# Norm sums collected while the residual is made, no meetings of the engines around norms, gate rows loaded aside, and one build of the rotation tables, in a three-block model kernel

## The chip, the cores and the metric

The kernel runs on one core of one Trainium2 chip. Five engines work side by side and meet only through semaphores: TensorE (PE, matrix products and transposes into PSUM), VectorE (DVE), ScalarE (ACT, which also starts the small loads), GpSimd (POOL, here mostly a queue of DMA starts) and SyncE (SP, here only the queue of weight loads). The metric is device microseconds for one execution. Less is better.

## The reference, cut to what matters

x is 1024 rows (time) by 1024 columns, float32. It passes three blocks. Between the large products stand norms over the 1024 columns of each row: five of the plain kind and three of the layer kind.

```python
def rmsnorm(x, g):                       # norm_g[0], norm_g[1], final_g, norm_w_3, final_norm_w_3
    return x * lax.rsqrt(jnp.mean(x * x, -1, keepdims=True) + 1e-6) * g

def _layer_norm(x, g, b):                # ln_in, ln1, ln2
    mu = jnp.mean(x, -1, keepdims=True)
    var = jnp.mean(jnp.square(x - mu), -1, keepdims=True)
    return (x - mu) * lax.rsqrt(var + 1e-5) * g + b

# block 1: an S5 mixer, then an SGU mixer
h = rmsnorm(x, norm_g[0]); branch, gate = split(h @ s5_w_in)
y = gelu(s5_mixer(branch, ...)); y = y * sigmoid(y @ s5_w_glu + b)
x = x + (y * silu(gate)) @ s5_w_out
h = rmsnorm(x, norm_g[1]); u, v, gate = split(h @ sgu_w_in)
x = x + (sgu_mixer(gelu(u), gelu(v), ...) * silu(gate)) @ sgu_w_out
x = rmsnorm(x, final_g)
# block 2
h = _layer_norm(x, ln_in_g, ln_in_b)
mix = concat([gated_delta(h @ w_in), forgetting_attention(h @ w_in)]) @ w_out
h = _layer_norm(ALPHA * h + mix, ln1_g, ln1_b)
ff = square(relu(h @ w_up)) @ w_down
ple = (p @ w_ple) * sigmoid(h @ w_ple_gate + b)
h = _layer_norm(ALPHA * h + ff + ple, ln2_g, ln2_b)
# block 3
h = _rmsnorm(h, norm_w_3); parts = h @ w_in_3 + b_in_3
x = h0 + concat([hgrn2(parts), gla(parts), mlstm(parts)]) @ w_out_3   # h0: what block 2 gave
out = _rmsnorm(x, final_norm_w_3)
```

In the S5 mixer a complex diagonal state of 64 groups is carried through time. The kernel does it with a real scan of blocks of 8 steps, for which the inputs are turned by powers of a unit complex number before the scan and turned back after it. These powers, 128 for each of 32 pairs of groups, are the rotation tables.

## The kernel before

All work is written out in order for each engine. The program is a list of 26 phases (from line 3167), and every engine runs its part of phase 1, then of phase 2, and so on. After every phase but the last stands `meet` (line 3190): each of the four computing engines drains, raises `phase_end`, and waits until all four have raised it. ACT starts the small loads of a phase first, then does its work in it (lines 3217 to 3220). SP alone runs ahead: it fills a ring of 8 weight blocks, waiting only for the product that frees a slot.

The residual stream lies in `c.X` as 8 tiles of 128 columns by 1024 rows, transposed (columns on partitions), so a mean over columns is a product with `mean_mat`, a 128x128 matrix of 1/1024. Products come as groups: `product_ct` (line 150) makes one tile of 128 columns by 1024 rows out of 8 tiles of input, 16 calls of 512 rows each. Each call shows as two matmul records in the trace, so a group is 32 records. There are two PSUM slots for groups. PE waits for a slot by `group_read`, the readers wait by `group_done`, and `taken` waits until a reader has read a group. The trace names `c.X` residual, `c.B` normed, `c.C` gate, `c.D` and the scratch areas work, `c.row` row.

`norm_phase` (line 196) is used for all eight norms. Plain kind: ACT squares tile k into one of two scratch tiles (line 230), PE multiplies it with `mean_mat`, summing over the 8 tiles in one PSUM group (line 220, 32 records), ACT makes the inverse root as exp(-0.5 ln) in `inverse_root` (lines 182 and 185, with a table load for each function), DVE scales all 8 tiles (line 248). Layer kind: PE first makes the mean the same way (line 213, 32 records), DVE copies it out of PSUM (line 240) and subtracts it tile by tile (line 243), then follow squares, sum, root and scaling as above, and DVE adds the bias in a second pass (line 253).

Ahead of a norm a phase makes the residual tile by tile: `load_phase` (transposes of x, copied out of PSUM by ACT and DVE in turn), `add_to_residual` (line 778, once per product group), `mix_phase` (line 1838) and `ff_phase` (lines 1932 to 1936). `rows3_phase` (line 1963), a phase of its own behind the last norm of block 2, loads 70 rows of gate parameters with 18 DMAs, turns them with one transpose and does six tiny steps.

The S5 mixer: `s5_input_phase` makes `branch` in 8 groups while DVE prepares parameters; `s5_scan_phase` (line 473) then makes 8 chunks of 8 groups of channels. In each chunk DVE builds two operand sets (lines 633 to 655, signal `s5_pq_done`), then the rotation table `E` of the chunk by doubling (lines 657 to 687), then, once PE has made `X` (line 574), turns, scans and turns back (lines 702 to 722, signal `s5_h_done`). PE in each chunk: transposes (line 554), kernel (line 566), `X` (line 574), one group of the gate product (line 158), then `y` (lines 584 and 586), which waits for `s5_h_done` and for a matrix that POOL sends through memory. ACT copies `y` out (line 606) before PE may begin the next chunk.

Of the kernel before, what the change touches and what calls it, by code (L numbers as in the profile page):

```python
# [16 lines left out]
P = 128  # L17
# [132 lines left out]
def product_ct(c, pe, g, blocks, acts):  # L150
# [12 lines left out]

def product_tc(c, pe, g, blocks, acts, tile):
# [3 lines left out]
    for q in range(0, len(blocks), 4):  # L168
# [4 lines left out]
        for k in range(KT):  # L173
            last = pe.matmul(out[:, q * P:q * P + BANK], acts[k][:, tile * P:(tile + 1) * P], wide[:, :, k, :],  # L174
# [12 lines left out]

def columns(c, w, first, count, k0=0, kt=KT):
# [7 lines left out]
def norm_phase(c, src, dst, gain, bias, eps):  # L196
# [3 lines left out]
    layer = bias is not None  # L200
    g_mean = c.plan.groups if layer else None
    c.plan.groups += 2 if layer else 1
    g_sq = c.plan.groups - 1
    scratch = c.tmp
    base = c.norms
    c.norms += 1

    def tensor(pe):
        if layer:
            out = start_group(c, pe, g_mean)  # L210
            for k in range(KT):
                for h in range(HALVES):
                    last = pe.matmul(out[:, h * BANK:(h + 1) * BANK], c.mean_mat[:, :],
                                     src[:, k, h * BANK:(h + 1) * BANK], start=(k == 0), stop=(k == KT - 1))
            last.then_inc(c.group_done, 1)
        out = start_group(c, pe, g_sq)
        for k in range(KT):
            pe.wait_ge(c.square_ready, KT * base + k + 1)
            for h in range(HALVES):
                last = pe.matmul(out[:, h * BANK:(h + 1) * BANK], c.mean_mat[:, :],  # L220
                                 scratch[:, k % 2, h * BANK:(h + 1) * BANK], start=(k == 0), stop=(k == KT - 1))
            last.then_inc(c.square_used if k < KT - 1 else c.group_done, 1)

    def scalar(act):
        for k in range(KT):
            if layer:
                act.wait_ge(c.centred, KT * c.layer_norms[g_sq] + k + 1)
            if k >= 2:
                act.wait_ge(c.square_used, (KT - 1) * base + k - 1)
            act.activation(scratch[:, k % 2, :], (dst if layer else src)[:, k, :], ACT.Square).then_inc(c.square_ready, 1)  # L230
        inverse_root(c, act, take_group(c, act, g_sq), bias=eps).then_inc(c.group_read[g_sq % 2], 1)

    if layer:
        c.layer_norms[g_sq] = len(c.layer_norms)

    def vector(dve):
        chain = c.dve_chain
        if layer:
            mean = take_group(c, dve, g_mean)
            chain.done(dve.tensor_copy(c.row[:, :], mean), c.group_read[(g_mean) % 2], (g_mean) // 2 + 1)  # L240
            chain.wait()
            for k in range(KT):
                dve.tensor_tensor(dst[:, k, :], src[:, k, :], c.row[:, :], ALU.subtract).then_inc(c.centred, 1)
            dve.wait_ge(c.centred, KT * (c.layer_norms[g_sq] + 1))
        taken(c, dve, g_sq)
        a = dst if layer else src
        for k in range(KT):
            chain.done(dve.scalar_tensor_tensor(dst[:, k, :], a[:, k, :], gain[:, k:k + 1], c.row[:, :],
                                                ALU.mult, ALU.mult))
        if layer:  # L250
            chain.wait()
            for k in range(KT):
                chain.done(dve.tensor_scalar(dst[:, k, :], dst[:, k, :], bias[:, k:k + 1], None, ALU.add))

    return Phase(tensor=tensor, scalar=scalar, vector=vector)


# [11 lines left out]
def load_phase(c, x):  # L269
# [20 lines left out]

    def scalar(act):
        for k in range(0, KT, 2):
            act.activation(c.X[:, k, :], take_group(c, act, g0 + k), ACT.Copy)\
               .then_inc(c.group_read[(g0 + k) % 2], 1)

    def vector(dve):
        dve.wait_ge(c.rows_turned, 1)
        dve.tensor_copy(c.vecs[:, 0:c.n_vector_rows], c.pb[:, 0, 0:c.n_vector_rows])
# [3 lines left out]
    return Phase(loads=loads, tensor=tensor, scalar=scalar, vector=vector)  # L302


def s5_input_phase(c, t):
# [38 lines left out]
    def tensor(pe):  # L344
# [4 lines left out]
        for m in range(KT):  # L349
            product_ct(c, pe, g0 + m, [(b0 + m, KT, P)], [c.B[:, k, :] for k in range(KT)])  # L350
# [118 lines left out]

    return Phase(loads=loads, tensor=tensor, scalar=scalar, vector=vector, gpsimd=gpsimd)  # L470


def s5_scan_phase(c, t):
# [30 lines left out]
    E = area(2, JC, S5_N)  # L504
# [84 lines left out]
    def scalar(act):  # L589
        for i in range(S5_C):  # L590
# [11 lines left out]
            act.activation(c.C[:, i, :], take_group(c, act, g0 + i), ACT.Silu).then_inc(c.group_read[(g0 + i) % 2], 1)  # L602
            act.wait_ge(c.s5_y_done, i + 1)
            if i >= 1:
                act.wait_ge(c.s5_y_stored, 16 * S5_T * i)
            act.activation(Y.rearrange("p (j e) n -> p e j n", e=2), c.pb[:, 2:4, :].rearrange("p e (j n) -> p e j n", j=JC), ACT.Copy)\
               .then_inc(c.s5_y_read, 1)

    def vector(dve):
# [7 lines left out]
        for i in range(S5_C):  # L617
# [4 lines left out]
            tmp = T.rearrange("p c j n -> p (c j n)")  # L622
            if i >= 1:
# [33 lines left out]
            ch.wait()  # L657
            ch.done(dve.memset(E[:, 0, :, 0:1], 1.0))
# [2628 lines left out]
```

## Time and profile before

| | us |
|---|---|
| median of 3 runs | 4812.77 |
| lowest, highest | 4812.63, 4816.57 |
| the profiled execution | 4816.69 |
| its span, first to last instruction | 4815.0 |
| PE busy in the span | 4298.4 (89%) |
| DVE, ACT, POOL busy | 1412.4, 850.3, 251.0 |
| mean granted TensorE clock | 0.93 of full |

In a row of the instructions in order of time stand: start and length in us, engine, line, operation, result<-operands, sizes, how many were merged. In brackets at the end is the idle time of that engine just before it and the engine and line that ended it. `DVEq L3193` or `ACTq L3193` is the `drain` of a `meet`. A granted clock of 1.00 is 2.4 GHz, 0.50 is 1.2 GHz.

### The profile page before, as it was taken

Reading aid. Unit: us, or ns where it says so; the run is one execution under the profiler, and the core shown is the slowest. Engines: PE = TensorE matmul, PEld = TensorE weight load, DVE = VectorE, ACT = ScalarE, POOL = GpSimd, SP = SyncE. Lnnn points to the kernel's source line nnn. Section 1 sums busy time; section 2 is a strip of 40 time slices with the busy share of each in tenths; the row PEclk is TensorE's granted clock in tenths of the full one; section 3 lists DMA queues with packets and bytes.
Section 4 is the critical chain, followed back from the end, with each engine's and each line's share of the span. In section 5 each row is a group of like instructions: output and inputs, shape, how many; then the busy total and the mean of one; then the engine's idle time right before and its main releaser. Section 6 shows DMA issues by size and latency. Waiting matters only on the chain. (4 is left out here: it accounts for less than half of the span.)

```text
span 4815.0 us, 32872 instructions
## 1 busy us (share of the span) xinstructions
PE 4298.4 (89%) x13735; PEld 2208.2 (46%) x13735; DVE 1412.4 (29%) x2443; ACT 850.3 (18%) x945; POOL 251.0 (5%) x368
## 2 busy tenths in 40 slices
PE   6888698999879899977989999999969999889787
PEld 3455343444344577444434444444425555444443
DVE  3388201210133454133110000000234553312432
ACT  2111101200125121243000000000032430210122
POOL 0133000000000122021000000000000000000000
PEclk9878799999979999988999999999989999979898
DMA  3122111111001111100111111111101001011000
GB/s 106 60 49 54 60 35 40 44 31 40 26 10 35 36 31 31 48 31 14 31 35 40 39 36 39 39 32 30 44 18 27 27 9 40 7 40 56 21 9 37
DMA packets 287985, 172.98 MB, mean 36 GB/s; under 512 B 24047, under 2 KB 278878, under 8 KB 287582
## 3 DMA queue, kind: packets, MB, share of 16 engines
q1 hardware_dynamic: 248848, 124.86, 9.3%
q0 software_dynamic: 9856, 23.87, 1.9%
q10 hardware_dynamic: 29134, 22.14, 1.5%
q8 instruction: 110, 1.80, 0.2%
q14 instruction: 37, 0.30, 0.0%
HBM read 157.63 MB, written 13.21 MB: 35 GB/s over the span
## 5 line engine op out<-in xcount | busy, mean ns | idle before, releaser
L158 PE MATMUL products<-normed,weights 128*128 128x512 f32 x2176 | 953.7, 599 | 46.5 <-ACT normed L748 36.5
L158 PE MATMUL products<-residual,weights 128*128 128x512 f32 x1696 | 736.3, 595 | 19.7 <-DVEq L3193 18.8
L158 PEld LDWEIGHTS products<-normed,weights 128*128 128x128 f32 x2176 | 416.3, 192 | 569.6 <-issue 561.0
L158 PE MATMUL products<-gate,weights 128*128 128x512 f32 x1408 | 613.9, 596 | 18.8 <-POOLq L3193 7.6
L158 PEld LDWEIGHTS products<-residual,weights 128*128 128x128 f32 x1696 | 323.3, 191 | 426.8 <-issue 403.3
L158 PEld LDWEIGHTS products<-gate,weights 128*128 128x128 f32 x1408 | 269.1, 191 | 360.9 <-issue 337.6
L2224 PE MATMUL products<-normed,weights 128*128 128x512 f32 (+1 forms) x672 | 306.4, 606 | 1.6 <-DVEq L3193 1.6
L2224 PEld LDWEIGHTS products<-normed,weights 128*128 128x128 f32 (+1 forms) x672 | 123.3, 190 | 148.3 <-issue 145.2
L174 PE MATMUL products<-weights,normed 128*128 128x512 f32 x384 | 167.6, 599 | 13.4 <-DVEq L3193 13.4
L614 DVE TENSOR_TENSOR work<-work 128x4 f32<-128x4 f32 (+9 forms) x592 | 171.4, 289 | 21.6 <-DVE work L661 0.5
L230 ACT ACTIVATE work<-residual 128x1024 f32<-128x1024 f32 x64 | 67.1, 1055 | 538.6 <-DVEq L3193 305.1
L220 PE MATMUL products<-work,mean_mat 128*128 128x512 f32 x256 | 123.9, 646 | 41.8 <-ACT work L230 41.8
L3003 POOL DMA_DIRECT2D out_dram<-work x8 | 4.3, 538 | 2564.0 <-ACT work L2992 2560.4
L781 DVE TENSOR_TENSOR residual<-products,residual 128x1024 f32<-128x1024 f32 x32 | 39.2, 1225 | 301.5 <-PE products L158 301.5
L174 PEld LDWEIGHTS products<-weights,normed 128*128 128x128 f32 x384 | 73.7, 193 | 106.9 <-issue 92.6
L2303 PEld LDWEIGHTS others<-work 128*128 128x128 f32 (+1 forms) x1024 | 94.4, 195 | 47.3 <-issue 37.9
L1497 PE MATMUL products<-residual,weights 128*128 128x512 f32 x256 | 115.9, 600 | 0.0
L2303 PE MATMUL others<-work 128*128 128x128 f32 (+1 forms) x1024 | 98.8, 283 | 17.6 <-DVE work L2491 5.7
L2237 PE MATMUL products<-weights,normed 128*128 128x512 f32 x256 | 111.5, 593 | 0.0
L220 PEld LDWEIGHTS products<-work,mean_mat 128*128 128x128 f32 x256 | 52.1, 207 | 113.0 <-issue 101.0
L1906 ACT ACTIVATE normed<-products 128x1024 f32<-128x1024 f32 x16 | 16.4, 1023 | 444.6 <-PE products L158 444.6
L158 PE MATMUL products<-work,weights 128*128 128x512 f32 x192 | 87.5, 606 | 4.9 <-POOLq L3193 4.9
(458 smaller groups left out, 4265.6 us busy)
## 6 DMA issues: line engine op xcount, KB each, us to landing
weights<-in_w_in_dram SPq DMA_DIRECT2D x80, 512.0 KB, 3.8
weights<-in_w_up_dram SPq DMA_DIRECT2D x32, 512.0 KB, 4.1
weights<-in_w_down_dram SPq DMA_DIRECT2D x32, 512.0 KB, 3.9
weights<-in_sgu_w_in_dram SPq DMA_DIRECT2D x24, 512.0 KB, 3.8
weights<-in_s_w_in_dram SPq DMA_DIRECT2D x16, 512.0 KB, 4.1
weights<-in_w_out_dram SPq DMA_DIRECT2D x24, 256.0 KB, 2.8
work<-in_x_dram ACTq DMA_DIRECT2D x8, 512.0 KB, 10.2
branch_scratch<-work POOLq DMA_DIRECT2D x8, 512.0 KB, 3.0
```

The lines of the kernel that those rows point to most:

```text
L158: last = pe.matmul(out[0:cols, half * BANK:(half + 1) * BANK], slot(c, b, kt, cols)[:, k, :], acts[n][:, half * BANK:(half + 1) * BANK], s ...
L174: last = pe.matmul(out[:, q * P:q * P + BANK], acts[k][:, tile * P:(tile + 1) * P], wide[:, :, k, :], start=(k == 0), stop=(k == KT - 1))
L220: last = pe.matmul(out[:, h * BANK:(h + 1) * BANK], c.mean_mat[:, :], scratch[:, k % 2, h * BANK:(h + 1) * BANK], start=(k == 0), stop=(k ...
L230: act.activation(scratch[:, k % 2, :], (dst if layer else src)[:, k, :], ACT.Square).then_inc(c.square_ready, 1)
L614: return ch.done(dve.tensor_tensor(o, a, b, op), signal)
L781: dve.tensor_tensor(c.X[:, m, :], take_group(c, dve, g + m), c.X[:, m, :], ALU.add)\
L1497: last = pe.matmul(o[:, 0:BANK], slot(c, f.b, KT, P)[:, kk, :], x[kk][:, half * BANK:(half + 1) * BANK], start=(kk == 0), stop=(kk == KT - 1))
L1906: act.activation(inner[m], take_group(c, act, g), ACT.Relu).then_inc(read, 1)
L2224: last = pe.matmul(out[0:cols, half * BANK:(half + 1) * BANK], slot(c, f.b, kt, cols)[:, kk, :], acts[kk][:, half * BANK:(half + 1) * BANK ...
L2237: last = pe.matmul(out[:, 0:BANK], x[kk][:, f.n * P:(f.n + 1) * P], wide[:, :, kk, :], start=(kk == 0), stop=(kk == KT - 1))
L2303: last = pe.matmul(pair(j + h)[:, i * P:(i + 1) * P], K[rows(u, h), i * P:(i + 1) * P], Q[rows(u, h), i * P:(i + 1) * P], start=True, stop ...
L3003: sp.dma_start(out[i * P:(i + 1) * P, :], stage[:, i, :]).then_inc(c.out_stored, 16)
```

## The change

Six things are done.

- While a phase makes the residual tile by tile, the sum that the next norm needs is collected in `c.total` (a new use of `c.W2[:, 0:1024]`): for plain norms (class `Sums`) ACT squares each tile and DVE adds the squares, for `ln1` and `ln2` (class `Means`) DVE adds the tiles. PE then makes the mean out of `c.total` with 2 calls in place of 16. The sum of squares within a layer norm, the mean of `ln_in` and the sum of squares of `norm_w_3` stay with PE, tile by tile.
- Each scaled tile raises `normed`, and the first group of the next product waits for tile k ahead of its k-th step. The meetings around norms go: of 25 there remain 10 (`meet=True`).
- In layer norms the subtraction reads the mean from PSUM without a copy, and the bias is added by ACT, tile by tile behind DVE's scaling. For `ln2` ACT also squares each finished tile for the norm after it.
- `rows3_phase` is no phase any more: its parts run inside `ff_phase`.
- The rotation tables are built once, for all 8 chunks, at the end of DVE's part of `s5_input_phase`, in `c.C`. In the scan ACT's silu into that tile of `c.C` moves behind the copy of `y`.
- The SGU's bias row is loaded into `c.row` only when all 8 tiles are normed.

```diff
-            if k < len(phases) - 1:
+            if k in meets:
@@ product_ct (product_tc and the first fill of decay_phase alike, store_phase for its first tile)
+            if ready is not None:
+                pe.wait_ge(c.normed, ready + n + 1)
@@ new
+class Sums:
+    def square(self, act, m):
+        if m >= 2:
+            act.wait_ge(c.collected, self.collected + max(1, m - 2))
+        act.activation(c.tmp[:, m % 2, :], c.X[:, m, :], ACT.Square).then_inc(c.square_ready, 1)
+    def collect(self, dve, m):
+        dve.wait_ge(c.square_ready, self.ready + m + 1)
+        c.dve_chain.wait()
+        first = c.tmp[:, 0, :] if m == 1 else c.total
+        c.dve_chain.done(dve.tensor_tensor(c.total, first, c.tmp[:, m % 2, :], ALU.add), c.collected)
+def mean_of_total(c, pe, g, collected):
+    out = start_group(c, pe, g)
+    pe.wait_ge(c.collected, collected + KT - 1)
+    for h in range(HALVES):
+        last = pe.matmul(out[:, h * BANK:(h + 1) * BANK], c.mean_mat[:, :], c.total[:, h * BANK:(h + 1) * BANK],
+                         start=True, stop=True)
+    last.then_inc(c.group_done, 1)
@@ ln_phase, scalar
+        for k in range(KT):
+            act.wait_ge(c.scaled, scaled + k + 1)
+            act.activation(dst[:, k, :], dst[:, k, :], ACT.Identity, bias=bias[:, k:k + 1]).then_inc(c.normed, 1)
+            if then_squares is not None and k:
+                act.wait_ge(c.normed, normed + k)
+                square_for_sum(c, act, dst[:, k - 1, :], k - 1, then_squares[1])
@@ load_phase, scalar
             act.activation(c.X[:, k, :], take_group(c, act, g0 + k), ACT.Copy)
+            for m in (k, k + 1):
+                taken(c, act, g0 + m)
+                sums.square(act, m)
@@ add_to_residual
         dve.tensor_tensor(c.X[:, m, :], take_group(c, dve, g + m), c.X[:, m, :], ALU.add)
+        if sums is not None and m >= 2:
+            sums.collect(dve, m - 1)
+    if sums is not None:
+        sums.collect(dve, KT - 1)
@@ s5_input_phase, vector (for all 32 pairs of groups; in the scan the same loop for 4 pairs goes)
+        while m < S5_N:
+            er, ei = E[:, 0, :, :, m // 2], E[:, 1, :, :, m // 2]
...
+                tt(E[:, n, :, :, m + 1:2 * m], a, b, op)
+            m *= 2
@@ sgu_phase, loads
+        sp.wait_ge(c.normed, normed + KT)
         sp.dma_start(bs, t["sgu_b_s"][0].rearrange("h t -> (h t)").partition_broadcast(P))
```

How the order moves at three places. On DVE at the end of the S5 gate phase, where the residual is made (residual<-products,residual) and the norm for the SGU follows (normed<-residual,vectors,row), before:

```order
L772 TENSOR_TENSOR gate<-gate,work 128x1024 [waits s5_gated,group_read1]
L781 TENSOR_TENSOR residual<-products,residual 128x1024 [waits group_done] x8
L248 SCALAR_TENSOR_TENSOR normed<-residual,vectors,row 128x1024 [waits group_read0,phase_end]
L248 SCALAR_TENSOR_TENSOR normed<-residual,vectors,row 128x1024 x7
L877 BN_STATS small<-work 128x6 [waits group_read1,params_loaded,phase_end]
```

and after (L228 is the adding of squares into the total):

```order
L916 TENSOR_TENSOR residual<-products,residual 128x1024 [waits group_done] x3
L228 TENSOR_TENSOR work<-work 128x1024 [waits s5_gated,square_ready]
L916 TENSOR_TENSOR residual<-products,residual 128x1024 [waits group_done]
L228 TENSOR_TENSOR work<-work 128x1024 [waits collected,square_ready]
...
L916 TENSOR_TENSOR residual<-products,residual 128x1024 [waits group_done]
L228 TENSOR_TENSOR work<-work 128x1024 [waits collected,square_ready] x2
L278 SCALAR_TENSOR_TENSOR normed<-residual,vectors,row 128x1024 [waits group_read0]
L278 SCALAR_TENSOR_TENSOR normed<-residual,vectors,row 128x1024 x7
```

The adding of squares stands between the residual adds, one tile behind, and the last two stand behind the last add; no wait for `phase_end` is left. On ACT from the end of `ff_phase` to the first work of `decay_phase` (L230 and L182, L185: squares and root), before:

```order
L1912 ACTIVATE work<-products,vectors 128x1024 [waits group_done,ple_added] x6
L230 ACTIVATE work<-residual 128x1024 [waits centred,phase_end]
L230 ACTIVATE work<-residual 128x1024 [waits centred]
L230 ACTIVATE work<-residual 128x1024 [waits square_used,centred] x6
L182 ACT_TABLE_LOAD
L182 ACTIVATE row<-products,eps 128x1024 [waits group_done]
L185 ACT_TABLE_LOAD
L185 ACTIVATE row<-row 128x1024 [waits act_step]
L230 ACTIVATE work<-residual 128x1024 [waits phase_end]
L230 ACTIVATE work<-residual 128x1024
L230 ACTIVATE work<-residual 128x1024 [waits square_used] x6
L182 ACT_TABLE_LOAD
```

and after, from the first root on (L351 is the bias, L301 a square):

```order
L189 ACTIVATE row<-row 128x1024 [waits act_step]
L351 ACTIVATE residual<-residual,vectors 128x1024 [waits scaled] x2
L301 ACTIVATE work<-residual 128x1024 [waits normed]
L351 ACTIVATE residual<-residual,vectors 128x1024 [waits scaled]
...
L301 ACTIVATE work<-residual 128x1024 [waits square_used,normed] x2
L186 ACT_TABLE_LOAD
L186 ACTIVATE row<-products,eps 128x1024 [waits group_done]
L189 ACT_TABLE_LOAD
L189 ACTIVATE row<-row 128x1024 [waits act_step]
L2387 DMA s_small<-in_b_in_dram 128x512
```

Bias and square of successive tiles alternate on ACT, and the 18 loads of gate rows that stood behind the second root are gone from here. On DVE in a chunk of the scan, between the operand sets and the turning (the table loop stands at L658 to L614 128x4x63, six doublings of which the last is shown), before:

```order
L614 TENSOR_TENSOR work<-work 128x4x4x16 x2
L658 MEMSET work 128x4
L659 MEMSET work 128x4
L661 COPY work<-s_small 128x4 x2
...
L614 TENSOR_TENSOR work<-work 128x252 x2
L614 TENSOR_TENSOR work<-work 128x4x63
L688 COPY work<-s_small 128x512
L690 MEMSET work 128x4
L614 TENSOR_TENSOR work<-s_small,ident 16x128
```

and after:

```order
L774 TENSOR_TENSOR work<-work 128x4x4x16 x2
L818 COPY work<-s_small 128x512
L820 MEMSET work 128x4
L774 TENSOR_TENSOR work<-s_small,ident 16x128
L829 TENSOR_TENSOR work<-work 16x8x16
L774 TENSOR_TENSOR work<-others,gate 128x512 x4
```

The 70 instructions of the table are gone from the chunk, and the turning reads the table from `gate`. 70 wider ones stand once at the end of DVE's part of `s5_input_phase`.

## Rows read from the trace of the kernel before

**Rows 1.** The page: span, and busy time, share and instructions of each engine.

```profile
span 4815.0 us, 32872 instructions
...
PE 4298.4 (89%) x13735; PEld 2208.2 (46%) x13735; DVE 1412.4 (29%) x2443; ACT 850.3 (18%) x945; POOL 251.0 (5%) x368
```

**Rows 2.** Instructions in order of time, S5 gate phase to SGU.

```profile
781.03 1.23 DVE L781 TENSOR_TENSOR residual<-products,residual 128x1024 f32<-128x1024 f32 x1 [12.51 <-PE products L158]
783.53 13.97 PE L220 MATMUL products<-work,mean_mat 128*128 128x512 f32 x32 [2.54 <-ACT work L230]
...
797.54 1.11 ACT L182 ACTIVATE row<-products,eps 128x1024 f32<-128x1024 f32 x1 [1.08 <-PE products L220]
...
801.14 9.66 DVE L248 SCALAR_TENSOR_TENSOR normed<-residual,vectors,row 128x1024 f32<-128x1024 f32 x8 [18.89 <-ACTq L3193]
810.90 29.68 PE L174 MATMUL products<-weights,normed 128*128 128x512 f32 x63 [13.40 <-DVEq L3193]
```

**Rows 3.** The same view, SGU phase to the input of the delta rule.

```profile
1282.33 1.22 DVE L781 TENSOR_TENSOR residual<-products,residual 128x1024 f32<-128x1024 f32 x1 [12.51 <-PE products L158]
...
1328.91 1.22 DVE L240 COPY row<-products 128x1024 f32<-128x1024 f32 x1 [16.83 <-PE products L213]
1330.16 9.17 DVE L243 TENSOR_TENSOR residual<-residual,row 128x1024 f32<-128x1024 f32 x8
...
1332.68 16.59 PE L220 MATMUL products<-work,mean_mat 128*128 128x512 f32 x32 [3.88 <-ACT work L230]
...
1362.59 5.39 DVE L253 TENSOR_SCALAR residual<-residual,vectors 128x1024 f32<-128x1024 f32 x8
...
1374.39 0.31 PE L976 MATMUL others<-ident,work 49*128 49x49 f32 x1 [25.11 <-DMA work<-in_b_f_dram]
```

**Rows 4.** The same view, around ln1.

```profile
2374.15 1.22 DVE L1838 SCALAR_TENSOR_TENSOR residual<-residual,products 128x1024 f32<-128x1024 f32 x1 [12.51 <-PE products L158]
...
2429.20 11.04 PE L158 MATMUL products<-residual,weights 128*128 128x512 f32 x20 [18.82 <-DVEq L3193]
```

**Rows 5.** The same view, last tile of ff_phase to first product of block 3.

```profile
3457.38 1.23 DVE L1932 TENSOR_TENSOR work<-products,work 128x1024 f32<-128x1024 f32 x1 [13.42 <-PE products L158]
...
3555.90 4.45 PE L2224 MATMUL products<-normed,weights 128*128 128x512 f32 x5 [1.62 <-DVEq L3193]
```

**Rows 6.** The same view, first transposes of the store.

```profile
4796.98 3.25 PE L2987 MATMUL products<-ident,residual 128*128 128x128 f32 x14 [13.38 <-DVEq L3193]
```

**Rows 7.** The same view, end of the load phase to the first product.

```profile
33.87 1.23 DVE L300 COPY residual<-products 128x1024 f32<-128x1024 f32 x1 [1.19 <-PE products L288]
...
55.67 9.66 DVE L248 SCALAR_TENSOR_TENSOR normed<-residual,vectors,row 128x1024 f32<-128x1024 f32 x8 [20.58 <-ACTq L3193]
...
69.55 10.69 PE L158 MATMUL products<-normed,weights 128*128 128x512 f32 x18
```

**Rows 8.** S5 scan: DVE instructions of line 614, who waited for them; us, times.

```profile
  PE others L584: 24.3, 8
```

**Rows 9.** The stretches in which PE makes `y`, windows view; columns stand first.

```profile
core 0: us, PE busy (x), PEclk, DMA share, GB/s
...
266.71:279.45 12.74, 12.74 (x48) 0.61 0.15 41
...
462.86:471.35 8.49, 8.49 (x48) 1.00 0.20 61
502.32:517.35 15.03, 15.03 (x48) 0.50 0.00 0
sum 109.17, PE 109.16; mean PE 13.64
```

**Rows 10.** Order of time, DVE: wait ahead of the scan, one table.

```profile
188.48 0.07 DVE L616 MEMSET work<- 128x8 f32 x1 [78.38 <-POOLq L3193]
...
237.83 0.17 DVE L661 COPY work<-s_small 128x4 f32<-128x4 f32 x1
...
251.60 2.70 DVE L614 TENSOR_TENSOR work<-work 128x252 f32<-128x252 f32 x6
...
254.22 0.42 DVE L688 COPY work<-s_small 128x512 f32<-128x512 f32 x1
```

More of the change, by code:

```diff
@@ new lines, in sum_squares, with square_for_sum @@
+def sum_squares(c, pe, g, ready, used):
+    out = start_group(c, pe, g)
+    for k in range(KT):
+        pe.wait_ge(c.square_ready, ready + k + 1)
+        for h in range(HALVES):
+            last = pe.matmul(out[:, h * BANK:(h + 1) * BANK], c.mean_mat[:, :], c.tmp[:, k % 2, h * BANK:(h + 1) * BANK],
+                             start=(k == 0), stop=(k == KT - 1))
+        last.then_inc(c.square_used if k < KT - 1 else c.group_done, 1)
+def square_for_sum(c, act, x, k, used):
+    if k >= 2:
+        act.wait_ge(c.square_used, used + k - 1)
+    act.activation(c.tmp[:, k % 2, :], x, ACT.Square).then_inc(c.square_ready, 1)
@@ new lines, in next_squares, with ln_phase, tensor @@
+def next_squares(c):
+    ready, used = c.n_squares, c.n_used
+    c.n_squares += KT
+    c.n_used += KT - 1
+    return ready, used
+def ln_phase(c, src, dst, gain, bias, means=None, after=None, squares_next=False):
+    g_mean = c.plan.groups
+    g_sq = g_mean + 1
+    c.plan.groups += 2
+    squared = next_squares(c)
+    then_squares = next_squares(c) if squares_next else None
+    normed, centred, scaled = c.n_normed, c.n_centred, c.n_scaled
+    c.n_normed += KT
+    c.n_centred += KT - 1
+    c.n_scaled += KT
+    def tensor(pe):
+        if means is not None:
+            mean_of_total(c, pe, g_mean, means.collected)
+        else:
@@ L215, in tensor @@
             last.then_inc(c.group_done, 1)
[L216 to L222, printed above, removed]
+        sum_squares(c, pe, g_sq, *squared)
@@ L236, in vector @@
-    def vector(dve):
[L237 to L244, printed above, removed]
+            if k < KT - 1:
+                act.wait_ge(c.centred, centred + k + 1)
+            else:
+                taken(c, act, g_mean)
@@ new lines, in scalar @@
+        if then_squares is not None:
+            act.wait_ge(c.normed, normed + KT)
+            square_for_sum(c, act, dst[:, KT - 1, :], KT - 1, then_squares[1])
+    def vector(dve):
+        ch = c.dve_chain
+        mean = take_group(c, dve, g_mean)
+        ch.wait()
+        for k in range(KT):
+            ins = dve.tensor_tensor(dst[:, k, :], src[:, k, :], mean, ALU.subtract)
+            if k < KT - 1:
+                ins.then_inc(c.centred, 1)
+            else:
+                ch.done(ins, c.group_read[g_mean % 2], g_mean // 2 + 1)
@@ L245, in vector @@
         taken(c, dve, g_sq)
-        a = dst if layer else src
+        ch.wait()
         for k in range(KT):
[L248 to L255, printed above, removed]
+            ch.done(dve.scalar_tensor_tensor(dst[:, k, :], dst[:, k, :], gain[:, k:k + 1], c.row[:, :], ALU.mult, ALU.mult),
+                    c.scaled)
@@ L737, in s5_gate_phase @@
     sig = c.tmp
+    sums = Sums(c)
     def loads(sp):
@@ new lines, in build @@
+        load = then(load_phase(c, t["x"][0]))
+        norm = then(rms_phase(c, c.X, c.B, c.vec["norm_g0"], sums=load.sums))
+        then(s5_input_phase(c, t, norm.normed), meet=True)
+        then(s5_scan_phase(c, t), meet=True)
+        gate = then(s5_gate_phase(c, t))
+        norm = then(rms_phase(c, c.X, c.B, c.vec["norm_g1"], sums=gate.sums))
+        sgu = then(sgu_phase(c, t, norm.normed))
+        norm = then(rms_phase(c, c.X, c.X, c.vec["final_g"], sums=sgu.sums))
+        norm = then(ln_phase(c, c.X, c.X, c.vec["ln_in_g_2"], c.vec["ln_in_b_2"], after=norm.normed))
```

295 lines of the change are left out of this document (184 added, 111 removed).

## The prediction

> **What bounds the kernel now.** I read the page first. PE is busy 4298.4 of 4815.0 us [rows 1], so the kernel is one queue of matrix work, and only two things count: PE work that goes away, and stretches in which PE stands still. The other engines have room on the whole (DVE 29%). So I went to the instructions in order of time and looked where PE stands still. There are seven such joints, at the norms, and one long stretch in which it runs below its pace, the S5 scan.
>
> One joint in detail [rows 2]. PE ends the last product at about 781.0. DVE's last residual add starts at 781.03. Only then do the squares begin, and PE sums them in 13.97 us. ACT's logarithm starts at 797.54. DVE scales from 801.14, 9.66 us for 8 tiles. PE's next product starts at 810.90, after 13.40 idle. From the last add that is 29.9 us, of which 20.1 lie ahead of the scaling and 9.8 are scaling and meeting. The same pattern stands at 1282.33 [rows 3] and at the final norm [rows 6].
>
> In the scan, the first `y` product of all 8 chunks was released by DVE, with 24.3 us of idle PE in sum [rows 8]. There DVE is the bound. A table takes it from 237.83 to 254.22, 16.4 us per chunk [rows 10].
>
> **The change, part by part.** All steps count from the start of the last residual add.
>
> Unit A, a plain norm whose squares are collected. The last add ends at 1.2. The sum of the last two squares comes behind it on DVE, two adds of the add's own kind, 1.23 us each [rows 2]; the last square on ACT hides behind the first of them. That makes 3.8. PE then has 2 calls, 4 records, where it had 32 in 13.97: 1.75 us. But it has then stood still for about 4 us, and a run of 32 records after 3.88 us of idle took 16.59 [rows 3] against 13.97 after 2.54 [rows 2], so it may start at half the clock. I take 3.5 us. Logarithm to scaling is 3.6 us as before (797.54 to 801.14). Scaling starts at 3.8 + 3.5 + 3.6 = 10.9, not 20.1: **9.2 us less** (11 at the full clock).
>
> Unit B, the start of the next product. It followed the start of scaling by 9.8 us, now by one tile (1.2) and a hand-over (0.1): **8.4 us less**. The 8 steps of the first group each take 1.75 us of PE, and scaling gives a tile every 1.21, so mostly PE sets the pace. The SGU's first steps have one call each (0.87) and wait for the tiles; half a microsecond goes there.
>
> *Load phase and norm_g0* [rows 7]: 33.87 (last copy) to 69.55 (product), of it 21.8 to the scaling. ACT now has 4 copies and 8 squares, DVE 4 copies and 7 adds, tied together through two scratch tiles. With 1.0 to 1.2 us for each, followed one by one, the total is ready 8.9 us behind the 33.87 mark, not at once. Mean 3, root 3.6: scaling starts at 15.5. The loads of S5 parameters start on ACT behind the root and now run during the scaling. The product still stands behind all 8 tiles, because the first transposes of that phase need a DVE copy queued behind the scaling: 9.7 + 1.0. So 26.2 in place of 35.7: 9.4 less (6 to 12; 12 if only DVE's own work counts, 6 if every hand-over of the scratch tiles adds a little).
>
> *norm_g1*: 9.2 + 8.4 - 0.5 = 17 less (15 to 20).
>
> *final_g and ln_in* [rows 3]: 1282.33 to 1374.39 is 92.1. Now: scaling at 10.9, mean of ln_in one tile later (12.2), 16.7 as before (16.83 was DVE's wait for it), 28.9. The copy (1.22) is gone. Subtract, square and hand-over 2.6, squares on PE 15.5 (between 14.0 and 16.59, since its idle ahead of them shrinks), root 3.6: 50.6. Scaling 9.7, last bias on ACT 1.2 in place of DVE's second pass of 5.39, loads of gate weights 6.4 as before: 67.9. 24 less (21 to 28).
>
> *ln1* [rows 4]: 55.05 before. Now add and one add into the total 2.6, mean 1.75 (PE idle under 3), 2.6 to the squares, 16.5, root 3.6, first tile scaled and biased 2.5, together 29.7: 25 less (23 to 28). ACT then has 19 loads to start, about 6 us, ahead of its first relu. The first group takes 16 us, so they just fit, and the second PSUM slot would give 13 us more.
>
> *ln2, norm_w_3, gate rows* [rows 5]: 98.5 before. Three DVE steps and one add 5.1, mean 3.5, 2.7, squares 16.5, root 3.6, first tile 2.4: 33.8. ACT then has bias and square for each tile, 2.25 us a tile, and PE (1.75 a tile) follows it: last square 50.7, sum ends 53. Root 3.6, one tile 1.3: 57.9. The gate rows' loads, transpose and two meetings are gone from this joint; in ff_phase their small steps lie beside products of 14 us. 40 less (36 to 44).
>
> *Final norm* [rows 6]: 9.2, and the first tile of transposes ends with the scaling instead of starting after it, 1.8: 11 less (9 to 13).
>
> *Scan.* DVE loses 16.4 us of some 39 per chunk, and nothing else in the chunk changes length. PE's own chain then rules: from the copy of `y` about 9 us of small steps, 13.8 of gate product, then `y`. DVE needs 11 us from `X` to `s5_h_done`, within the 13.8. POOL has 8 stores, 8 loads and the matrix through memory, some 17 us behind the copy of `y`, against 22. So the 24.3 us of waiting go [rows 8]. The length of `y` follows the clock: 12.74 us at 0.61 after hardly any idle, 8.49 at 1.00, 15.03 at 0.50 after the longest idle, in sum 109.17 [rows 9]. Without the wait I take the nearest row, 12.74: 101.9, 7.3 less. 32 less in all (13 if all eight take 15.03, 66 if all take 8.49).
>
> *The single table build.* It is added to DVE in `s5_input_phase`, which has 78.38 us idle there before the scan [rows 10]. 36 wide operations with 23,040 elements in sum, 34 others. From 2.70/6 = 0.45 us for 252 elements and 1.23 for 1024, it is 0.19 plus 1.0 ns an element: 30 us, and 7 for the small ones, 37 us. Hidden by PE's eight groups; beyond 78 us each one would count in full.
>
> A rule and this trace: the subtraction from SBUF takes 9.17/8 = 1.15 us, an add out of PSUM 1.23 [rows 2, 3]. The Trainium skill, VectorE: DVE Perf Modes, Rules for kernel authors, advises to copy a product out of PSUM first when many operations follow. By that rule dropping the copy is a mistake; by the rows eight reads lose 0.6 us and all but the first lie beside PE's squares, while the copy was 1.25 us on the path. By the rule the three layer norms would give back about 4 us.
>
> **Sum**: 9.4 + 17 + 24 + 25 + 40 + 11 + 32 = 158.4 us. The profiled execution took 4816.69, of it 1.7 outside the span, and lies 3.9 above the median. Against the median: 4812.8 - 158.4 = 4654.
>
> **The rivals.**
> 1. *PE stays slow in `y`.* At 0.50 in all chunks the scan gives 13: 4673. For it: five of eight stretches lay at 0.54 or below. Against: those followed longer waits.
> 2. *Another wait takes over in the scan* (the matrix through memory). It would need 5 us more than I count in POOL's queue per chunk. The scan then gives little: 4686.
> 3. *Full clock in `y`*: without pauses PE keeps 1.00 as in the seventh chunk, which had hardly waited either: 4621.
> 4. *The joints give only the PE work*, since tile-by-tile hand-overs stall: no unit B at four joints, 34 us lost: 4688.
> 5. *Slower.* The products behind the joints stay at 1.2 GHz, because their first steps now come with a wait each. A group of 32 records takes 13.7 us at the full clock and 27.4 at half, so each group so run costs 13.7. From 12 groups on the gain is gone, with 16 it is 4873. Against: the first product after a joint recovers within its first group (20 records in 11.04 us where 8.6 would do) [rows 4], and only its first steps carry waits.
>
> **How the numbers follow.** Forecast 0.66; rival 1 0.12, rival 2 0.05, rival 3 0.11, rival 4 0.04, rival 5 0.02. The forecast's own bounds without the scan are 111 to 145 around 126, so with the scan's 32 about 4635 to 4670. The range reaches to rival 3 on one side and to 2 and 4 on the other: 4612 to 4690. About 0.2% is what a measurement of this kernel can tell from no change, 10 us; only rival 5 gets there. Faster 0.975, same 0.005, slower 0.02.
>
> **What would show it.** In the profile after: at each plain norm PE's mean has 4 records, and the next product starts some 12 us behind the last add (29.9 before). The joint of ln2 and norm_w_3 is 58 us long. In the scan the wait for DVE ahead of `y` is near zero and the chunks follow at some 36 us. DVE ends its tables well before PE's eighth group. The forecast is wrong if `y` waits for POOL's matrix, if ACT's bias-and-square pace is over 3 us a tile, or if products after the joints show a granted clock near 0.5 for more than one group.

## The result, and the profile after

The changed kernel takes **4607.4 us** (median of 4 runs, 4602.5 to 4610.6), the kernel before 4812.7 (4 runs beside it, 4809.2 to 4816.6). The ratio is 0.9575, with a 95% interval of 0.9563 to 0.9587. The forecast was 4654, range 4612 to 4690: right in direction, 47 us too high, and 5 us outside the range.

First lines of the page after, to be held against [rows 1]:

```profile
span 4608.8 us, 32069 instructions
...
PE 4185.0 (91%) x13567; PEld 2145.3 (47%) x13567; DVE 1366.2 (30%) x1968; ACT 875.9 (19%) x969; POOL 250.9 (5%) x368
```

PE is busy 113 us less, with 168 records fewer. These are six sums that had 32 records and now have 4, and together they explain some 70 us. The rest is work that is still there and runs faster.

The joint of norm_g1 in order of time, to be held against [rows 2]:

```profile
697.45 1.23 DVE L916 TENSOR_TENSOR residual<-products,residual 128x1024 f32<-128x1024 f32 x1 [11.38 <-PE products L160]
698.59 2.54 DVE L228 TENSOR_TENSOR work<-work 128x1024 f32<-128x1024 f32 x2
...
701.28 2.48 PE L251 MATMUL products<-work,mean_mat 128*128 128x512 f32 x4 [3.87 <-DVE work L228]
703.80 1.11 ACT L186 ACTIVATE row<-products,eps 128x1024 f32<-128x1024 f32 x1 [2.73 <-PE products L251]
...
707.31 9.65 DVE L278 SCALAR_TENSOR_TENSOR normed<-residual,vectors,row 128x1024 f32<-128x1024 f32 x8 [6.17 <-ACT row L189]
708.74 11.55 PE L178 MATMUL products<-weights,normed 128*128 128x512 f32 x21 [4.98 <-DVE normed L278]
```

From the last add to the scaling are 9.9 us (20.1 before), to the product 11.3 (29.9 before). Both units of the prediction can be seen: four records for the mean, and a product that starts 1.4 us behind the scaling.

The scan. PE's stretches of `y`, windows view, against [rows 9]:

```profile
core 0: us, PE busy (x), PEclk, DMA share, GB/s
211.21:219.63 8.42, 8.42 (x49) 1.00 0.22 64
...
427.31:435.73 8.42, 8.42 (x49) 1.00 0.21 62
sum 67.36, PE 67.34; mean PE 8.42
```

All eight are 8.42 us long at the full clock (2.4 GHz), in sum 67.4 where they were 109.2. One chunk around them, PE in order of time:

```profile
282.89 1.94 PE L714 MATMUL others<-ident,work 128*128 128x128 f32 x8 [1.21 <-ACT work L765]
284.76 2.60 PE L726 MATMUL others<-work,s_small 64*16 64x128 f32 x32
288.48 1.97 PE L734 MATMUL others<-work 128*64 128x128 f32 x32 [1.12 <-ACT work L759]
290.37 14.00 PE L160 MATMUL products<-normed,weights 128*128 128x512 f32 x32
304.21 0.38 PE L744 MATMUL others<-work 128*128 128x128 f32 x2
```

The last line has no bracket: PE goes from the gate product into `y` without a pause. `y` starts every 30.9 us (39.3 before). From the first transposes to the end of the last `y` the scan takes 246.7 us; before it was 318.4.

Stage by stage, from the two traces, in us less than before:

| stage | predicted | measured |
|---|---|---|
| load, norm_g0 | 9.4 | 9 to 9.9 |
| scan | 32 | **72** |
| S5 gate phase | 0 | 2 |
| norm_g1 | 17 | 18.6 |
| final_g, ln_in | 24 | 25.5 |
| ln1 | 25 | 26.1 |
| ln2, norm_w_3, gate rows | 40 | 41.8 |
| final norm, store | 11 | 10 |
| sum | 158.4 | 205 |

Six of the seven predicted terms are within 2 us. The scan alone makes 40 of the 47 us.

### The profile page after: what moved, and what is told of

The parts are those of the page before. It is cut to its first block and busy times, and to the rows that moved or that the text cites. A ratio compares the mean times of both kernels' runs of the same rounds, so it can differ in the third digit from the quotient of the medians.

```text
span 4608.8 us, 32069 instructions
## 1 busy us (share of the span) xinstructions
PE 4185.0 (91%) x13567; PEld 2145.3 (47%) x13567; DVE 1366.2 (30%) x1968; ACT 875.9 (19%) x969; POOL 250.9 (5%) x368
## 5 line engine op out<-in xcount | busy, mean ns | idle before, releaser
L221 ACT ACTIVATE work<-residual 128x1024 f32<-128x1024 f32 x32 | 33.7, 1057 | 269.2 <-DVE residual L916 230.6
L2669 DVE COPY_PREDICATED work<-levels,others 128x1024 f32<-128x1024 int32 x56 | 73.0, 1304 | 36.9 <-PE others L2481 32.2
L2525 ACT ACTIVATE work<-work 128x1024 f32<-128x1024 f32 x48 | 50.5, 1054 | 161.5 <-DVE work L2648 119.0
L2089 DVE TENSOR_TENSOR gate<-gate 128x1024 f32<-128x1024 f32 x16 | 19.6, 1224 | 200.1 <-ACT gate L2073 200.1
## 6 DMA issues: line engine op xcount, KB each, us to landing
work<-in_x_dram ACTq DMA_DIRECT2D x8, 512.0 KB, 10.2
```

Source lines behind the costliest of these rows:

```text
L221: act.activation(c.tmp[:, m % 2, :], c.X[:, m, :], ACT.Square).then_inc(c.square_ready, 1)
L2525: act.activation(E[l % 4], E[l % 4], ACT.Exp).then_inc(c.decay_exp, 1)
L2669: ch.done(dve.copy_predicated(o, mask, got), *reader(j))
```

## The experiments

**Theory.** The tables lay in VectorE's loop, and that loop set the chunk before. With them gone PE's own loop sets it, and since PE no longer stands still ahead of `y`, its clock stays at 2.4 GHz there. **Rivals:** the higher clock has another cause (Silu's new place, the sum of idle time in a chunk, VectorE's load), or the low clock had already been a cost of its own before.

The runs of the kernel before that stand beside these kernels have medians of 4809.1 to 4812.4, so a difference between kernels that ran apart is good to some 4 us. Two single traces can differ by more: one stretch that no experiment touches, the forgetting attention of block 2, takes 204.7 us in the trace of the changed kernel and between 198.5 and 208.3 us in the 14 traces at hand.

### The tables, out and in

Of the change only this, put into the kernel before (with Silu moved, which now has to clear the tables' buffer last); and the reverse, in the changed kernel:

```
+        E = c.C.rearrange("p i (c j n) -> p c i j n", c=2, j=S5_JC)
+        sets = [P, S5_C, S5_JC]
...
-            ch.done(dve.memset(E[:, 0, :, 0:1], 1.0))
-            ch.done(dve.memset(E[:, 1, :, 0:1], 0.0))
...
```

> The kernel before with one part of the change: tables built once, and Silu moved. Theory: chunks of 30.9 us, `y` 8.5 us at clock 1.00, 72 us less: 4741 (4737 to 4746), and the rest of the change is then worth 133. Rival (the full clock in `y` needs something else of the change, the barrier or the sums ahead of it): `y` at 12 to 15 us, chunks of 35 to 37, the time 4768 to 4785, which is what the prediction had given this part (32 less).

Measured: 4738.9 us (4735.5 to 4741.9), ratio 0.9854 (0.9839 to 0.9868); 71.2 below the runs of before on the same chip (4810.1). `y` is 8.42 us in all eight chunks.

> The changed kernel with the rotation tables built in each chunk again, as before; the new place of Silu, the sums and the missing barriers stay. Theory (the tables alone made the scan 72 us shorter: they took 16.4 us of VectorE's loop of 39.8 us a chunk, and without its wait TensorE runs `y` at the full clock): the chunk is 39.8 us again, the scan 318 us, `y` 11 to 15 us long at a granted clock below 0.8, the time 4607 + 72 less the 2 or 3 us by which VectorE's table build before the scan gets shorter, in no one's way: 4677 to 4682. Rival (Silu behind the copy of `y`, or the other start of the scan, gave a part of it): the chunk stays 1 us or more below 39.8 and the time below 4672.

Measured: 4676.5 us (4672.8 to 4680.5), 69 above the changed kernel. The chunk is 39.1 us and the scan 317.6; before they were 39.3 and 318.4, and the 39.8 of my expectation was off. Seven `y` take 12.9 to 15.1 us, the seventh of the eight 8.5 at a clock of 1.00, against my expectation. Lines of the first pairs of `y` in one chunk, order of time:

```profile
375.37 0.49 PE L718 MATMUL others<-work 128*128 128x128 f32 x2 [2.60 <-DVE work L748]
...
376.43 0.71 PE L718 MATMUL others<-work 128*128 128x128 f32 x2
...
378.22 0.79 PE L718 MATMUL others<-work 128*128 128x128 f32 x2
```

After 2.60 us of standing still the same pair of matmuls goes from 0.49 to 0.79 us within 3 us: the clock falls inside `y`, behind the pause and not ahead of it. The two runs agree: the tables are worth 69 to 71 us. Silu's new place without the single build brings nothing beyond the scatter, nor does the joint ahead of the scan. Silu can't stay in its old place when the tables lie in `c.C`, so no run has the single build without the move.

### Where PE stands still

Six repeats of one multiplication (0.71 us each) in each chunk of the changed kernel, once ahead of the signal for `y` (first piece), once ahead of that for the transposes (second):

```
+            for _ in range(6):
+                tt(v(T2[:, 1]), v(Hh[:, 0]), v(E[:, 1]), ALU.mult)
```
```
+            for _ in range(6):
+                tt(o0, dr, bc(Br), ALU.mult)
```

> The changed kernel with one multiplication of 508 columns done seven times instead of once in each chunk, behind the scan and ahead of the signal that `y` waits for: 6 x 0.71 = 4.3 us more on VectorE, of which 2.6 us are covered, so TensorE waits about 1.7 us ahead of `y`. Theory (TensorE's clock in `y` falls when a wait stands ahead of it): `y` goes from 8.5 to 12 us or more at a clock near 0.6, the chunk grows by the wait and by 3.5 to 6.5 us more: 41 to 65 us in all, 4648 to 4672. Rival (the clock in `y` has another cause, and the wait costs its own length): `y` stays 8.5 us, 8 x 1.7 = 14 us more, 4621.

Measured: 4664.1 us (4662.6 to 4667.2), 56.7 more. Its `y`, two starts in order of time and the windows:

```profile
328.50 0.49 PE L744 MATMUL others<-work 128*128 128x128 f32 x2 [1.60 <-DVE work L774]
...
366.76 0.49 PE L744 MATMUL others<-work 128*128 128x128 f32 x2 [1.59 <-DVE work L774]
```
```profile
328.50:342.64 14.14, 14.13 (x48) 0.54 0.12 35
366.76:375.28 8.52, 8.52 (x48) 1.00 0.17 50
...
sum 105.72, PE 105.70; mean PE 13.21
```

The wait is 1.53 to 1.60 us in all eight chunks, so 12.7 in sum. `y` grew by 38.4 (105.7 - 67.4), three times the wait, and the matrix steps behind it by some 4. Seven stretches ran at 0.53 to 0.59, one at 1.00 behind the same wait.

> The same 4.3 us of repeated VectorE work in each chunk, but at its start, ahead of the signal that the transposes of the next chunk wait for; 1.9 us are covered there, so TensorE stands still 2.4 us longer behind `y` and not ahead of it. Theory (place decides: the 14 us product between that wait and `y` keeps the clock up): `y` stays at 8.5 us and clock 1.00, 8 x 2.4 = 19 us more, 4626. Rival (the sum of idle time in a chunk decides, wherever it lies): `y` goes to 12 us or more as in the other run, 47 to 71 us more, 4654 to 4678.

Measured: 4633.5 us (4631.9 to 4635.9), 26.0 more, 7.5 over what I gave.

```profile
330.39 1.97 PE L714 MATMUL others<-ident,work 128*128 128x128 f32 x8 [3.77 <-DVE work L774]
332.29 3.18 PE L726 MATMUL others<-work,s_small 64*16 64x128 f32 x32
```
```profile
318.20:326.62 8.42, 8.42 (x49) 1.00 0.21 62
...
sum 67.36, PE 67.34; mean PE 8.42
```

Here PE stands still 3.77 us, longer than in the run before it, and no `y` is touched: a 14 us product lies between. The cost is the wait (7 x 2.56 = 18), 4 in the slower small steps (the matrix 3.18 instead of 2.60), and some 5 ahead of the first chunk; I had left out the last two. By these two runs the place of the pause decides, not the sum of idle time.

> As the run with six repeats ahead of `y`, but with four: 1.59 us of waiting less 2 x 0.71 leaves 0.1 to 0.2 us ahead of `y`. Theory (the clock falls behind a wait that is long enough, and the 0.46 us of one chunk before was enough): with 0.2 us `y` stays at 8.4 to 8.5 us and full clock in most chunks, 1 to 2 us in all, 4609. Rival (any wait at all brings the clock down): `y` at 13 to 14 us in most chunks, 35 to 45 us more, 4642 to 4652.

Measured: 4619.1 us (4614.8 to 4623.6), 11.7 more; the profiled run's span is 4613.0, 4.2 more. The wait ahead of `y` is 0.15 us in four chunks and not to be seen in the others, and `y` is 8.52 us at 1.00 in all eight. That the clock holds is as expected. The time is 10 us over what I gave: 0.7 us a chunk come from transposes that wait 1.88 us for DVE instead of 1.21 for ACT, the rest is not explained (the median lies 4 us above the profiled run).

### Useless work in place of standing still

If it is the pause that costs, filling it with matmuls whose result is overwritten must pay (two of them here, nine in the kernel before):

```
+            for _ in range(2):
+                pe.matmul(pt[:, 0:BANK], c.ident[:, :], c.B[:, 0, 0:BANK], start=True, stop=True)
             pe.wait_ge(c.s5_h_done, i + 1)
```

> The kernel with six repeats ahead of `y` (4664), and two matmuls of 512 columns, whose result `y` overwrites, between the gate product and the wait for `y`: 2 x 0.87 = 1.74 us of TensorE work in place of 1.59 us of standing still. Theory (standing still ahead of `y` is what takes the clock down): `y` 8.4 to 8.5 us at clock 1.00 in all chunks, the chunk then 33.6 us as in the one undisturbed chunk of that run, 21 us above the changed kernel: 4628 (4624 to 4634), 36 us faster than without the useless work. Rival (the added VectorE work or the longer chunk takes it down, not the standing still): `y` stays at 13 to 14 us, and the two matmuls cost nothing or 1 to 2 us: 4664 to 4667.

Measured: 4631.2 us (4630.4 to 4634.5): 16 matmuls more, and **33 us less** than 4664.1. Windows of `y`:

```profile
315.32:323.84 8.52, 8.52 (x49) 1.00 0.18 55
...
sum 68.15, PE 68.14; mean PE 8.52
```

VectorE's load is that of the slow run, so its load is not the cause.

> The kernel before, with nine such useless matmuls (7.8 us) ahead of the wait for `y`. Theory (in the kernel before VectorE's loop of 39.2 us set the chunk, and TensorE's low clock in `y` lay in its shadow): `y` falls from 15.03 or 12.74 to 8.5 us at clock 1.00, `y` in sum from 109 to 68, and the time stays within 4 us of 4812. Rival (the low clock in `y` was on the path, as the prediction counted it: a term of its own beside the waits): 30 to 40 us less, 4772 to 4782.

Measured: 4809.7 us (4805.1 to 4813.5) against 4809.1, ratio 1.0001 (0.9991 to 1.0010).

```profile
303.69:312.22 8.53, 8.52 (x48) 1.00 0.01 2
...
383.32:391.74 8.42, 8.42 (x49) 1.00 0.00 0
...
sum 67.63, PE 67.61; mean PE 8.45
```

`y` is 41.5 us shorter than in [rows 9], and the time does not move. So the low clock cost nothing before. VectorE's loop of 39.3 us hid it. It is with the tables gone that the clock decides. Two of the eight `y` still have a wait ahead of them, 0.98 us (the first line) and 0.95, and they too run at 1.00.

### The joints

Barriers behind every phase again (but for the one between ln2 and norm_w_3):

```
-        def then(phase, meet=False):
+        def then(phase, meet=True):
```

> The changed kernel with a barrier behind every phase again, but for the one between ln2 and norm_w_3, whose squares now belong to both; the sums tile by tile, the bias on ScalarE, the gate rows aside and the tables stay. Theory (the prediction's unit B: with a barrier the product behind a norm starts 8 scaled tiles later instead of one, 8.4 us): five joints have it in full, the product behind norm_g1, the mean of ln_in, the products behind ln1 and norm_w_3, the transposes of the store: 5 x 8.4 = 42, and some ten barriers at about 0.5 us: 4607 + 47 = 4654 (4648 to 4660). Rival 1 (the early start gained little, since the tiles come in at 1.2 us and the first product only waits inside itself instead of ahead): under 20 us in all, 4612 to 4627. Rival 2 (the longer idle ahead of each product also drops TensorE's clock in it, 13.7 us for a group): over 80 us more, above 4687.

Measured: 4653.7 us (4647.2 to 4657.7), 46.3 more. Its list of PE's waits shows unit B, against 4.98 to 4.99 us for the first two in the changed kernel:

```profile
PE products L178 <- DVEq L3392: 14.7, 1, 14.7
PE products L336 <- DVEq L3392: 14.7, 1, 14.7
PE products L3171 <- DVEq L3392: 14.7, 1, 14.7
```

By the starts of the next PE step: norm_g1 9 us, ln_in 9, ln1 8, norm_w_3 10, the first joint 5. At the store the first transposes come 10 to 11 us later but need not wait for single tiles afterwards, and 4 remain. The sum was right; the equal shares were not.

Sums of squares by matmul behind the last tile again, at four norms, without barriers:

```
+            for k in range(KT):
+                taken(c, act, last + k)
+                square_for_sum(c, act, src[:, k, :], k, squared[1])
```

> The changed kernel with the sums of squares of norm_g0, norm_g1, final_g and the final norm done as before by 16 matmuls behind the last tile, from squares that ScalarE makes once a tile of the residual is done; no barriers. Theory (the prediction's unit A: these sums cost 20.1 us from the last add to the scaling, against 10.9): 4 x 9.2 = 37 at most, less some 2 us at each joint, since without a barrier the first squares and matmuls now start ahead of the last add: 26 to 37, 4633 to 4644. Rival (the missing barrier alone hides them, the squares run beside the adds as in the sums tile by tile): under 12 us in all, below 4619.

Measured: 4632.0 us (4623.2 to 4634.5), 24.5 more, slightly under my bounds. The next product came 8 us later at norm_g1 and final_g, but only 3 at norm_g0 and 5 at the final norm. There the squares and matmuls start well ahead of the last tile once no barrier stands between. These shares are read at the joints: the whole span of this trace is only 12.7 us longer, because between 1192 and 2124 us it regains 8 in instructions that the edit does not touch. The range of the runs, 11 us, is the measure of how well 24.5 is known.

> The changed kernel with the rows of gates loaded, transposed and worked in a phase of their own between norm_w_3 and block 3, with a barrier behind it, as before. Theory (the prediction counted them as a part of the 40 us of that joint): before they took from 3546.7, the end of the scaling, to 3555.9, and the first product can't start on the first scaled tile: 9 to 12 us more, 4616 to 4619. Rival (they cost as much where they lie now, since ScalarE starts 19 loads ahead of its first relu and TensorE waits for it): no difference, 4605 to 4609.

```
-        ff = then(ff_phase(c, t, norm.normed, rows3_phase(c, t)))
+        ff = then(ff_phase(c, t, norm.normed, None))
...
+        then(rows3_phase(c, t), meet=True)
```

Measured: 4617.5 us (4616.2 to 4623.3), 10.1 more. Block 3's first product starts at 3369.78 instead of 3358.82. In ff_phase the rows cost nothing that can be seen.

### What was still to be had

The four row loads of the S5 parameters moved to the first phase, the seven loads of the gdn input to final_g, both on GpSimd:

```
+    def gpsimd(sp):
+        for n, name in enumerate(("s5_A_re", "s5_A_im")):
...
+        def early(pool):
+            pool.wait_ge(c.normed, final.normed + 1)
+            gdn.early(pool)
```

> The changed kernel with the two waits taken away that its trace still shows at a norm's product: the four row loads of the S5 parameters are issued by GpSimd during the first phase, and VectorE's copy of them comes ahead of the scaling, so the first S5 product can start on the first scaled tile (51.5 instead of 60.5 us); the seven loads of the gdn input phase are issued by GpSimd at final_g, so its first matmuls start on the first tile with its bias (about 1233 instead of 1246.4), bounded by the last bias for the first of 8 token tiles. Theory: 9 us and 8 us less, 17 in all: 4590 (4586 to 4596). Rival (what stands behind these loads is late as well: ScalarE's exponentials and sines of the S5 parameters hold up the third product, or the matmuls run at half the clock when they start between the biases): one of the two gives nothing, 4598 to 4607.

Measured: **4587.8 us** (4586.9 to 4597.4), ratio to before 0.9538 (0.9522 to 0.9554): 20 us below the changed kernel.

```profile
52.03 10.54 PE L160 MATMUL products<-normed,weights 128*128 128x512 f32 x17 [4.62 <-DVE normed L278]
...
1222.75 0.61 PE L1138 MATMUL others<-normed,residual 128*128 128x16 f32 x2 [5.89 <-ACT residual L351]
```

The S5 product starts at 52.03 instead of 60.53, and the gate weights' matmuls go along with the biases; that joint gives 10.8 us.

> The kernel with the loads early (4588), and one useless matmul (0.87 us) behind `y` in each chunk but the last, in the 1.21 us in which TensorE waits for the copy of `y`. Theory: the transposes and the kernel matrix behind it (1.94 and 2.60 us in the changed kernel at a granted clock of 0.80, 1.06 and 1.93 in a chunk with the clock at 1.00) keep the full clock: 1.5 us less in 7 chunks, 10 in all, 4578 (4575 to 4582). Rival (0.35 us of standing still that is left, or the small matmuls themselves, take it down all the same): 4586 to 4589.

```
+            if i < S5_C - 1:
+                pe.matmul(c.pb[:, 0, :], c.ident[:, :], c.B[:, 0, 0:BANK], start=True, stop=True)
```

Measured: 4585.9 us (4582.1 to 4587.0), 2 us less, inside the scatter, and above the 4575 to 4582 I gave.

```profile
241.88 1.06 PE L718 MATMUL others<-ident,work 128*128 128x128 f32 x8
242.88 1.94 PE L730 MATMUL others<-work,s_small 64*16 64x128 f32 x32
```

In the scan the theory holds: the small steps run at the full clock, a chunk takes 29.41 us, and the scan 236.1 instead of 244.0. But of these 8 us some 5 are given back between 2020 and 2250, in the same instructions. Most of that lies in the forgetting attention, 203.9 us without the filling and 208.1 with it. Since this stretch scatters by 10 us over the traces, it can't be put down to the filling; what moves it is open.

## Why the prediction was wrong

1. **What bounds the kernel: right.** One queue of PE, with joints. The table of stages above has each of the joints within 2 us.
2. **Unit A: right in size, 9.2 against 10.2 at norm_g1.** The mean took 3.54 and 3.75 us at final_g and the final norm, as I had taken, 2.48 at norm_g1. By single experiment the four sums gave 24.5, not 4 x 9.2 = 37: part of what I gave to unit A is owed to the missing barrier, without which early squares can start.
3. **Unit B: right,** 8 to 10 us at four joints, 46.3 in all with the barriers themselves. Rivals 4 and 5 are out: the joints gave unit B, and the products behind them did not stay at 1.2 GHz (at norm_g1 the granted clock is 0.82 in the first 11.6 us and 1.00 in the next 30).
4. **Gate rows: right,** 10.1 us by the run. Relu was not late: the rows' loads end at 2286.8, the first group at about 2288.
5. **Single table build: right.** It takes 39 us (37 estimated) and its last operation ends at 131.3, 41 us before the end of PE's eighth group; DVE's idle time ahead of the scan fell from 78.38 [rows 10] to 47.29.
6. **A rule on PSUM.** Dropping the copy cost nothing: the eight subtractions with the mean read from PSUM took 9.14 us, and 9.17 from SBUF [rows 3]. By the Trainium skill, VectorE: DVE Perf Modes, Rules for kernel authors, the copy should have stayed; this trace does not agree, with 0.03 us less over eight reads.
7. **Scan: the step that failed.** It is the size of one term, the length of `y`: "Without the wait I take the nearest row, 12.74", 7.3 us less in all. It measured 8.42 in every chunk, 41.8 us less. The wait itself went as forecast, 24.3 us, and rivals 1 and 2 are out: no `y` is at 0.50, and none waits for POOL's matrix. I took a row behind a pause for a kernel without one. Two rows of the kernel before, the starts of the second and the seventh `y`:

```profile
266.71 0.49 PE L584 MATMUL others<-work 128*128 128x128 f32 x2 [0.46 <-DVE work L614]
...
462.86 0.49 PE L584 MATMUL others<-work 128*128 128x128 f32 x2 [1.20 <-DVE work L614]
```

The first `y` took 12.74 us, and I read its 0.46 us as "hardly any idle"; the second took 8.49, and I called 1.20 us hardly a wait too. Together they said that the length of the pause does not fix the clock, and no row showed a `y` without a pause. (Also, six of the eight stretches lay at 0.54 or below, not five.) The six-repeat run shows that a pause of 1.6 us is enough for 13 to 14.5 us in seven of eight chunks, the four-repeat run that with 0.15 us or none `y` takes 8.5. Rival 3, with a chance of 0.11, was the case that came true. It gave 66 us; of the 6 more, 3 are the matrix steps behind `y`, in sum 21.6 us where they were 24.9.
8. **The form of the sum: right.** A wait that goes (24.3) and a `y` that shrinks both shorten PE's own chunk, and both count once VectorE's loop is no longer the longest. As a maximum of two loops: DVE's 39.3 us before, PE's after, which is 22.5 us of other steps plus `y`. With 12.74 that is 35.2, or 33 us in eight chunks, the same count as my 32. With 8.42 it is 30.9: seven steps of 8.4 us make 59, the first `y` starts 6.4 us sooner behind the first transposes, and the last is 6.6 us shorter, 72 in all. What the sum of waits does not show is the condition, and the kernel before filled shows it: there a shorter `y` alone is worth nothing.

What each part is worth alone: tables 70, barriers 46, the four sums 24, gate rows 10, together 150 of 205, if they add, which no run shows. The rest (the sums of the layer norms' tiles, the bias on ACT, the mean read where it stands) was not undone singly, so it is only argued from the traces.

Not settled: which chunks keep the clock. Behind equal waits of 1.53 to 1.60 us one of eight did. In the kernel before one with 1.20 us did while those with 0.46 and 1.24 did not, and in the kernel before filled, behind nine matmuls without use, those with 0.98 and 0.95 did. The runs show that a pause ahead of `y` brings the low clock in most chunks and that filling it takes the low clock away; they do not show the rule by which it falls.

## What to carry to other kernels

Write the cost of a pipelined loop as the longest of the engines' own loops, each with its own clock: a step made shorter counts only in the longest. When a change takes a pause away, don't take the length of the step behind it from a row that has a pause, however short. Ahead of many small matmuls a pause of 1.6 us cost three times its length on top of itself; give the other engine its slack there, or put the pause where few small steps and then a long dense product follow. There 18 us of waiting cost 4 us more in the small steps and nothing in `y`. Where a pause can't be avoided, a few matmuls without use may be cheaper than standing still (33 us here), but only if TensorE's loop is the longest (nothing in the kernel before).

## What the runs showed of the hardware

- With standing still of 1.53 to 1.60 us ahead of `y` (48 small records a chunk), the granted clock in it was 0.53 to 0.59 in seven of eight chunks; with none, 1.00 in all eight chunks of the changed kernel. The Trainium skill, TensorE: Matmul & The Clock Gate, What's actually happening, says that "the default state is throttled, and activity releases the throttle". The traces agree: with two matmuls without use in place of the pause the clock held in all eight, and behind nine of them it held over the 0.98 and 0.95 us that were left of two waits (8.53 us at 1.00).
- A wait of 3.77 us ahead of three small steps left the 14 us product (14.00 us) and `y` behind it (8.42 us, 1.00) at full clock, and slowed only the first two of the steps: 1.97 and 3.18 us, where 1.06 and 1.94 are the values with the pause filled.
- The same instructions take a different time from trace to trace where small matmuls alternate with waits: the forgetting attention of block 2 (812 or 813 matmul records) took 198.5 us at a granted clock of 0.91 in the run with barriers and 208.3 at 0.86 in the kernel before filled, 204.7 at 0.88 in the changed kernel.
